# ScalarE instead of GpSimd reads the page numbers and starts the cached k pages

## What is computed

```python
p = _rmsnorm(x, rms_mix_w) @ w_in            # att q|k|v, gdn q|k|v, z, a, b
att = attend(q_att, k_att, v_att)            # 8 heads x 128
gdn, s_new, gconv_new = _gated_deltanet(...) # 8 heads x 128
x = x + jnp.concatenate([att, gdn], axis=-1) @ w_out
f, fconv_new = _conv_ffn(_rmsnorm(x, rms_ffn_w), w_up, ...)
return x + f, ...
```

```python
cache_k, cache_v (DEPTH, N_POOL, PAGE_SIZE, N_ATT_HEADS, HEAD_DIM)   # paged K/V pool
page_table (DEC_BATCH, N_PAGES) int32                                # logical -> physical page
```

## Time and profile before

| | |
|---|---|
| median of three runs | 1661.22 us (1660.48 to 1662.82) |
| the profiled execution, its own time | 1660.96 us |
| its span, first to last instruction | 1659.3 us |
| TensorE busy in the span | 1636.3 us, 99% |
| VectorE, ScalarE, GpSimd busy | 63%, 37%, 14% |
| mean granted TensorE clock | 0.999 |
| DMA | 255.13 MB, 154 GB/s on average |

### The profile page before, as it was taken

One profiled execution on the slowest core, in us unless ns is written; L12 is line 12 of the kernel. 1 busy time (PEld: TensorE's weight loads), 2 busy tenths in 40 slices (PEclk: granted clock), 3 DMA queues, 4 the chain that ended last, 5 costly groups with the idle time before them and its releaser, 6 DMA issues.

```text
span 1659.3 us, 30938 instructions
## 1 busy us (share of the span) xinstructions
PE 1636.3 (99%) x12907; PEld 1584.9 (96%) x12907; DVE 1049.6 (63%) x1709; ACT 617.5 (37%) x786; POOL 236.2 (14%) x369
## 2 busy tenths in 40 slices
PE   7999999999999999999999999999999999999997
PEld 7999989988998998999999999999999999999997
DVE  5676688656544455676666666666666666666665
ACT  6444323432343343643333333333333333333334
POOL 1121342123202012210001010101010101010004
PEclk9999999999999999999999999999999999999999
DMA  8443355345846567444444444444444444544442
GB/s 240 129 116 108 114 141 165 103 121 154 271 149 217 166 204 224 134 152 153 153 152 147 147 151 153 152 145 149 152 152 150 145 151 145 160 141 153 152 153 84
DMA packets 230540, 255.13 MB, mean 154 GB/s; under 512 B 9085, under 2 KB 220607, under 8 KB 230401
## 3 DMA queue, kind: packets, MB, share of 16 engines
q1 hardware_dynamic: 217856, 220.16, 43.6%
q0 software_dynamic: 9856, 31.71, 6.1%
q10 hardware_dynamic: 2688, 1.27, 0.3%
HBM read 242.00 MB, written 11.12 MB: 153 GB/s over the span
## 4 chain that ended last, share of the span: by engine, by line
PE 93%; DVE 2%; DMA 2%; issue 1%; ACT 1%; SPq 0%; POOL 0%; DVEq 0%; POOLq 0%; ACTq 0%
PE ps_proj L1761 22%; PE ps_proj L1762 21%; PE ps_proj L1763 21%; PE ps_small L1761 6%; PE ps_small L1762 6%; PE ps_small L1763 6%; PE ps_small L1803 2%; DMA k_pages<-in_cache_k_dram 1%; DMA w_raw<-in_w_in_dram 1%; PE ps_small L1942 0%; PE ps_small L2032 0%; PE ps_small L1932 0%; DMA state_s<-in_state_gdn_dram 0%; DVE w_lo L1163 0%; PE ps_small L2007 0%
## 5 line engine op out<-in xcount | busy, mean ns | idle before, releaser
L1761 PE MATMUL ps_proj<-x_hi,w_hi 128*128 128x320 f32 x2432 | 767.7, 316 | 0.9 <-DVE x_lo L1279 0.5
L1762 PE MATMUL ps_proj<-x_lo,w_hi 128*128 128x320 f32 x2432 | 751.9, 309 | 0.0
L1763 PE MATMUL ps_proj<-x_hi,w_lo 128*128 128x320 f32 x2432 | 751.9, 309 | 0.0
L812 ACT ACTIVATE w_hi<-w_raw 128x1024 fp32r<-128x1024 f32 x408 | 431.9, 1059 | 746.3 <-PE ps_proj L1763 551.7
L1163 DVE TENSOR_TENSOR w_lo<-w_raw,w_hi 128x1024 fp32r<-128x1024 f32 x408 | 497.9, 1223 | 307.4 <-ACT w_hi L812 307.1
L1761 PEld LDWEIGHTS ps_proj<-x_hi,w_hi 128*128 128x128 f32 x2432 | 457.1, 188 | 15.9 <-issue 11.9
L1762 PEld LDWEIGHTS ps_proj<-x_lo,w_hi 128*128 128x128 f32 x2432 | 457.4, 188 | 1.3 <-issue 1.2
L1763 PEld LDWEIGHTS ps_proj<-x_hi,w_lo 128*128 128x128 f32 x2432 | 457.0, 188 | 0.0
L1761 PE MATMUL ps_small<-hid_hi,w_hi 128*128 128x320 f32 x704 | 218.0, 310 | 0.0
L1763 PE MATMUL ps_small<-hid_hi,w_lo 128*128 128x320 f32 x704 | 217.6, 309 | 0.0
L1762 PE MATMUL ps_small<-hid_lo,w_hi 128*128 128x320 f32 x704 | 217.5, 309 | 0.0
(11 more groups left out here) (348 smaller groups left out, 1216.8 us busy)
## 6 DMA issues: line engine op xcount, KB each, us to landing
w_raw<-in_w_up_dram SPq DMA_DIRECT2D x176, 512.0 KB, 3.6
w_raw<-in_w_in_dram SPq DMA_DIRECT2D x112, 512.0 KB, 3.8
w_raw<-in_w_down_dram SPq DMA_DIRECT2D x88, 512.0 KB, 3.5
w_raw<-in_w_out_dram SPq DMA_DIRECT2D x32, 512.0 KB, 4.2
k_pages<-in_cache_k_dram POOLq DMA_DIRECT2D x32, 256.0 KB, 3.6
v_pages<-in_cache_v_dram POOLq DMA_DIRECT2D x32, 256.0 KB, 4.1
state_s<-in_state_gdn_dram POOLq DMA_DIRECT2D x10, 512.0 KB, 5.8
out_ss_dram<-state_s POOLq DMA_DIRECT2D x8, 512.0 KB, 4.5
```

The source lines that it names most:

```text
L812: act.activation(whi[:, slot], raw[:, slot], ACT.Copy).then_inc(hi_done, 1)
L1761: pe.matmul(o, hi, rhs_hi[:, k0 + kk_, :], start=first and kk_ == 0, stop=False)
L1762: pe.matmul(o, hi, rhs_lo[:, k0 + kk_, :], start=False, stop=False)
L1763: ins = pe.matmul(o, lo, rhs_hi[:, k0 + kk_, :], start=False, stop=last and kk_ == CQ - 1)
```

## The change

`pk` becomes a step of ScalarE. `pk` 0 and 1 of a group move from the head of the group's list to the place behind its third `kv`. For each of the two pages ScalarE reads the number and starts the transfer, one page after the other; the wait for `kt` b - 2 stands ahead of both. The waits of group 0's first pages are gathered there (page table in DRAM read, the last state update, five older transfers out).

```diff
 def att_steps(g):
-    s = ([("G", "hk", g)] if g else []) + [("G", "pk", g, 0), ("G", "pk", g, 1)]
+    s = [("G", "hk", g)] if g else []
     s += [("P", "hk", g), ("V", "hk", g), ("P", "hb", g), ("V", "hb", g)]
     for t in range(3):
         s += [("P", "kv", g, t), ("A", "kv", g, t), ("G", "kv", g, t)]
-    s += [("G", "pv", g, 2), ("G", "pv", g, 0), ("G", "pv", g, 1), ("G", "pv", g, 3)]
+    s += [("A", "pk", g, 0), ("A", "pk", g, 1), ("G", "pv", g, 2), ("G", "pv", g, 0), ("G", "pv", g, 1), ("G", "pv", g, 3)]
...
             if b < DB - 2:
-                s += [("G", "pk", g, b + 2)]
+                s += [("A", "pk", g, b + 2)]
...
+                elif name == "pk":
+                    g, b = k
+                    if (g, b) == (0, 0):
+                        act.wait_ge(pt_in, 16)
+                        after(act, "V", "us", 1, 3)
+                        act.wait_ge(st_out, 32)
+                        for i in range(3):
+                            act.wait_ge(s_out[i], 16 * (2, 4, 2)[i])
+                    elif b > 1 or g:
+                        after(act, "P", "kt", *((g, b - 2) if b > 1 else (0, DB - 2 + b)))
+                    for i in range(2):
+                        page = act.value_load(ptab[0:1, 2 * b + i:2 * b + i + 1], min_val=0, max_val=n_pool - 1)
+                        src = I["cache_k"][0].rearrange("n s h d -> n s (h d)")[bass.DynSlice(page, 1), :, 512 * g:512 * g + 512]
+                        act.dma_start(kp[:, b % 2, i].rearrange("p h d -> p (h d)"), src.rearrange("a s c -> (a s) c"))\
+                            .then_inc(pk_in[b % 2], 16)
```

More of the change, by code:

```diff
@@ L409, in tallies @@
         for x in SLOTS[at_]:
-            if (x[0] == "G" and x[1] in TRANSFERS) or x[1] == "fload":
+            if (x[0] == "G" and x[1] in TRANSFERS) or x[1] in ("fload", "pk"):
                 continue
@@ L2404, in step @@
                         pool.dma_start(out, tile_).then_inc(kv_out[(3 * g + t) % 2], 16)
-                elif name in ("pk", "pv"):
+                elif name == "pv":
                     g, b = k
-                    if (g, name, b) == (0, "pk", 0):
-                        pool.wait_ge(pt_in, 16)
                     page = [pool.value_load(ptab[0:1, 2 * b + i:2 * b + i + 1], min_val=0, max_val=n_pool - 1) for i in range(2)]
[L2410 to L2425, removed]
+                    slot = b % 4
+                    if b > 3 or g:
+                        after(pool, "P", "PV", *((g, 0) if b > 3 else (0, 1)))
+                    if b == 3:
+                        after(pool, "P", "hk", g)
+                    if (g, b) == (0, 2):
                         pool.wait_ge(gs_out, 16 * 7)
-                    elif (g, name, b) == (0, "pv", 0):
+                    elif (g, b) == (0, 0):
                         after(pool, "V", "us", 1, 3)
@@ L2431, in step @@
                     for i in range(2):
-                        src = cache[0].rearrange("n s h d -> n s (h d)")[bass.DynSlice(page[i], 1), :, 512 * g:512 * g + 512]
-                        pool.dma_start(tile_[:, slot, i].rearrange("p h d -> p (h d)"), src.rearrange("a s c -> (a s) c"))\
-                            .then_inc(arrived[slot], 16)
+                        src = I["cache_v"][0].rearrange("n s h d -> n s (h d)")[bass.DynSlice(page[i], 1), :, 512 * g:512 * g + 512]
+                        pool.dma_start(vp[:, slot, i].rearrange("p h d -> p (h d)"), src.rearrange("a s c -> (a s) c"))\
+                            .then_inc(pv_in[slot], 16)
                 elif name == "qz":
```

## The result

The changed kernel takes 1664.8 us (median of 20 runs, 1662.37 to 1668.03), the kernel before 1660.64 us (20 runs, 1658.07 to 1663.11). The ratio is 1.0026, 95% interval 1.002 to 1.0032: 4.2 us slower, just over the 0.2% that can be told from no change. The profiled execution took 1663.73 us with a span of 1662.1 us, 2.8 us more than the one of before and 1.1 us under its own median, so a single trace need not show all of the 4.2 us.

A forecast was written before the change was run, and what follows sets the result against it. TensorE, busy 1636.3 of 1659.3 us, was taken as the bound, so new waits add one for one. Terms 1.7 + 0.6 + 0.3 + 0.6 + 1.8 - 1.0 = +4.0 us gave a median of 1665.2 us, range 1661.0 to 1671.0.

The forecast's parts named there:

- the side given 0.52: Whole kernel: the change makes it slower by over 0.2%, chance 0.52; same had 0.47, faster 0.01.
- the 4.28 us: ScalarE's queue, kernel before: eight starts at 643.23 kept the copies of `PT` waiting 4.28 us, until 647.73.
- A page's price: ScalarE's queue: read 0.55, register work 0.07, start 0.5, together 1.12 us a page; bounds 0.9 to 1.37.
- First `T` of group 1: Four pages ahead of the exponent delay the division; TensorE waits 1.7 us (0.9 to 2.7).
- `kt` 3 of group 0: Turns of group 0: pages start at 499.54, land in 3.45 us; TensorE waits 0.6 us (0.2 to 1.9).
- Other pairs: Other page pairs in the turns: second start 0.4 us later; 0.3 us of waits in all (0 to 1.0).
- `SS` 5 of group 1: `pk` 6 behind the parameter starts delays copies of `PT` and `kt` 5; TensorE waits 0.6 us (0 to 1.1).
- `kt` 6 of group 1: Its pages start at 649.4, land in 6.1 us; TensorE waits 1.8 us (0 to 2.8).
- Old page waits: TensorE's three waits for k pages in the kernel before go, -1.0 us.
- The hardware queue lands pages sooner: Rival, chance 0.27: pages started by ScalarE land in 3.0 us or less; +1.7 us, 1662.9.
- The reads wait for ScalarE's own work: Rival, chance 0.11: loads on this queue run only once ScalarE is idle; +8.6 us, 1669.8.
- No wait at all: Rival, chance 0.07: below 0.69 us a page the first `T` and the pairs cost nothing; -1.0 us, 1660.2.

The follow-up runs named there:

- the combined kernel: The change with group 1's first two pages begun at the group's head, page numbers read ahead, parameter rows started by GpSimd: 1660.18 us, 0.9993 of the kernel before.

## Why the prediction was right

The forecast, 1665.2 us with a sum of +4.0 us, came out at 1664.8 us and +4.2 us, on the side given 0.52, and by its mechanism: what stands behind a read and a start on ScalarE is held up. Of the earlier trace rows the prediction read too much: 1.64 us of the 4.28 us were the queue's, the rest was TensorE's turn of `PT`. The sum doesn't use the 4.28. The steps:

- **A page's price.** Taken at 1.12 us; measured 1.05 us from one start of a pair to the next (493.14 and 494.19 us). The read was taken rightly, 0.55 us for a measured 0.53. The start was taken too high, 0.34 us for the 0.5.
- **First `T` of group 1.** 1.7 us forecast, 1.62 us measured; gone with GpSimd's queue and with the pages begun early, 2.9 and 5.5 us with more reads. The closeness is partly luck: the exponent began 4.87 us after `kv` 2's first copy where 4.57 were forecast, 0.55 us of it for one slow load that nothing forecast, and `T` itself was due 0.3 us later behind that copy than before (5.07 for 4.78 us). In the three other traces with the same order here the wait was 1.58, 1.45 and 1.73 us, and one load of the four took 0.54 to 0.58 us.
- **`kt` 3 of group 0.** 0.6 us forecast, 1.13 us measured (1.0 to 1.4 in the later kernels that left it as it is). The start was right: 499.54 - 0.90 (this trace is that much ahead) = 498.64 us, measured 498.6. The landing was mis-sized, 4.1 us for 3.45.
- **Other pairs.** 0.3 us forecast, 0.53 us measured, and at another pair than I looked at: `kt` 7 of group 0, not one of group 1 that had waited before. The second start came 1.73 us after the copy's (499.26 and 500.99 us), as forecast.
- **`SS` 5 of group 1.** 0.6 us forecast, 0.78 us measured. It took the parameter starts and the pages' reads together: without either it was gone.
- **`kt` 6 of group 1.** This term failed: 1.8 us forecast, 0.29 us measured. The time of the start was nearly right: the parameter starts ended at 649.72 us, 2.1 us later than before, and the second page's start came 2.06 us behind that, for a forecast 1.75. `kt` 6 was due at 656.13 us, 0.2 us later than forecast (653.7, and 2.2 us by which this place had moved besides the six products). What was mis-sized is the landing, 4.6 us for the 6.1 of the earlier trace rows, 1.5 us sooner. Why isn't shown. It is not a free moment: the DMA share was 1.01 and 1.08 in 652 to 654 and 654 to 656 us, as high as in 648 to 654 us before (0.92, 1.05 and 0.96). It isn't ScalarE's queue alone either: there landings took 5.3 us in 645 to 650 with the numbers read ahead and 6.1 us in 640 to 645 in the combined kernel.
- **Old page waits.** They went, -0.98 us.

The terms' errors (-0.1, +0.5, +0.2, +0.2, -1.5) nearly cancel: the waits of the trace add 3.4 us where I had 4.0. That the median is so near the forecast is luck in part, as it grew by 4.2 us, and the 0.5 us between 4.2 and the 3.7 us from `kt` 0 isn't explained by one trace of each kernel.

**The rivals.** *The hardware queue lands pages sooner* is true by about 0.3 us on average, not by the 0.6 us and more that this rival needs: at `kt` 3 of group 0, where it has a wait of 0.15 us, TensorE waited 1.13 us. At `kt` 6 its 0.2 us lie nearer the measured 0.29 us than the forecast's 1.8. The Trainium skill (DMA: Bandwidth & Descriptors, section "Latency and other measured facts") gives the hardware path 0.4 us of lead to the first byte; the landings of these loaded transfers of 256 KB have about 0.3 us of it. *The reads wait for ScalarE's own work* didn't happen: the first load for the four pages began at 597.6 us, inside the copy of 597.53, the first start at 598.29, inside that of 598.03, and nothing near +8.6 us was seen. *No wait at all* needed a page under 0.69 us. The measured 1.05 us is above it, and the time came back when the pages went to GpSimd, or when pages, reads and rows went away from what is urgent. The same section's floor of 600 ns for a tensor_load isn't borne out as time on the queue: the load took 0.28 us as a rule on either queue and a whole read 0.53 us on ScalarE, though single loads on ScalarE took up to 0.85 us.

## What to carry to other kernels

Starting transfers on an engine's queue is free only by what stands behind them: ask for the next instruction on that queue that the bounding engine needs, and put reads of dynamic addresses ahead of a wait rather than between the wait and the start. An engine at 37% can be late and one at 14% be at its limit: compare the price of one item on the queue with the slack of one turn, since a lateness beyond it adds up. When a step is moved in time, take its landing from the time to which it goes, not from where it stood.

## Not expected

- **A long wait costs clock as well.** Behind a wait of 5.5 us TensorE ran at the lower level in the records until 612 to 614 us, 2.6 us of extra time. A lower clock also followed the waits of 2.94 and 1.96 us with the numbers read twice; with waits of up to 1.62 us, in the change, it stayed at 1.00. But it also fell near 114 us in two traces without any wait, 1.7 us of clock each time: two single executions can differ by that much for no reason of the edit.
- **GpSimd's slack is small in the turns.** It is 14% busy over the span, yet of a turn of 3.35 us its queue had only about 1.1 us left (3.35 less 1.13 for two starts and 1.1 for two reads), and two more reads for each pair used them up.
- **A landing time belongs to its moment.** The same 256 KB took 2.6 to 6.6 us in the change, all on one queue.
- **A load can be slow.** In the change four of the 32 loads of page numbers on ScalarE took 0.49 to 0.85 us instead of 0.28, one of them ahead of the exponent. They occur on GpSimd's queue as well (up to 0.53 us in the kernel before, 0.90 us where it read each number twice). The cause is not shown.
